# A two-block forward pass: the down products of the experts in four passes of 256 columns, with three quarters of the second block's projections under them

## The reference, cut to what matters

```python
hid = silu(einsum('becd,edf->becf', xs, w_gate)) * einsum('becd,edf->becf', xs, w_up)
eo  = einsum('becf,efd->becd', hid, w_down)          # w_down: 16 x 2048 x 1024
x   = x + zeros.at[bidx, idx].add(gates * eo)
x   = rms_norm(x, final_g)                           # end of the first block
h   = modulate(rmsnorm(x, g_pre_mix), shift, scale)  # start of the second
q, k, v, z, gl = split_proj(h @ w_in_2)              # 1024 x 7168
kv_c = hc @ w_in_2[:, 1024:3072]                     # keys and values of 256 context tokens
```

## Time and profile before

| | us |
|---|---|
| median of 2 timed runs (2216.74 to 2218.97) | 2217.85 |
| the profiled execution | 2217.74 |
| its span, first to last instruction | 2215.9 |
| PE busy | 1514.1 |
| DVE busy | 742.5 |
| ACT busy | 429.9 |
| mean transfer rate over the span, GB/s | 361 |

### The profile page before, as it was taken

The page is one execution under the profiler, slowest core; times in us unless marked ns, Lnnn a source line. Parts: engine busy times, 40 slices in busy tenths (PEclk is TensorE's granted clock), DMA queues, the critical chain, the costliest instruction groups (busy, mean ns, idle before and its releaser), DMA issues.

```text
span 2215.9 us, 24722 instructions
## 1 busy us (share of the span) xinstructions
PE 1514.1 (68%) x10356; PEld 613.8 (28%) x10356; DVE 742.5 (34%) x1862; ACT 429.9 (19%) x998; POOL 309.4 (14%) x290
## 2 busy tenths in 40 slices
PE   9998676776565655659855988897686854434445
PEld 7554133221111111113211334454333620100001
DVE  5831100000000000000000235445767686776774
ACT  1430100000000000000000106443414542221222
POOL 0110000000000000000000000001343445444351
PEclk9999888877777777889977999898686975565555
DMA  9699989999999999999455824357999999999997
GB/s 408 269 423 383 421 348 399 402 392 428 427 429 428 428 428 427 428 420 425 197 232 232 335 88 176 114 190 293 382 418 416 421 420 420 421 421 420 421 420 308
DMA packets 76750, 800.89 MB, mean 361 GB/s; under 512 B 9088, under 2 KB 9216, under 8 KB 10592
## 3 DMA queue, kind: packets, MB, share of 16 engines
q1 hardware_dynamic: 39008, 530.66, 57.4%
q0 software_dynamic: 37632, 268.65, 29.3%
HBM read 798.03 MB, written 1.05 MB: 361 GB/s over the span
## 4 chain that ended last, share of the span: by engine, by line
DMA 42%; PE 42%; DVE 9%; ACT 3%; issue 2%; POOL 0%; SPq 0%; DVEq 0%; another core or an unknown queue 0%; ACTq 0%; POOLq 0%
DMA AR<-in_peer_uv,AR 13%; DMA AR<-in_w_up 12%; DMA AR<-in_w_down 10%; PE PS L413 5%; DMA AR<-in_w_gate 5%; PE PS L699 5%; PE PS L860 5%; PE PS L772 5%; PE PS L424 4%; PE PS L738 4%; DVE AR L1638 3%; PE PS L996 3%; PE PS L953 2%; PE PS L535 1%; PE PS L781 1%
## 5 line engine op out<-in xcount | busy, mean ns | idle before, releaser
L699 PE MATMUL PS<-AR 128*32 128x512 f32 x2048 | 330.1, 782 | 202.9 <-DMA AR<-in_w_up 129.3
L2072 POOL DMA_INDIRECT AR<-in_peer_uv,AR x256 | 293.6, 1147 | 1071.8 <-DVE AR L1629 772.7
L996 PE MATMUL PS<-AR 32*32 32x512 f32 x4032 | 224.7, 907 | 288.5 <-ACT AR L2008 285.2
L1638 DVE CUSTOM_DVE_ANT_0 AR<-AR 128x1024 f32<-128x1024 f32 x256 | 309.2, 1222 | 158.8 <-DMA AR<-in_peer_uv,AR 158.2
L738 PE MATMUL PS<-AR 128*32 128x512 f32 x1024 | 177.9, 756 | 131.4 <-DMA AR<-in_w_down 130.8
L1292 DVE TENSOR_TENSOR AR<-AR,PS 128x512 f32<-128x512 f32 x16 | 11.0, 687 | 593.4 <-PE PS L699 593.4
L699 PEld LDWEIGHTS PS<-AR 128*32 128x32 f32 x2048 | 64.7, 127 | 447.0 <-DMA AR<-in_w_up 208.8
L996 PEld LDWEIGHTS PS<-AR 32*32 32x32 f32 x4032 | 39.1, 124 | 428.8 <-ACT AR L2008 415.2
L413 PE MATMUL PS<-AR 128*128 128x512 f32 x288 | 136.1, 629 | 7.3 <-ACT AR L1704 4.0
L1320 DVE COPY AR<-PS 128x512 f32<-128x512 f32 x8 | 5.5, 692 | 315.8 <-PE PS L738 315.8
L860 PE MATMUL PS<-AR 128*128 128x512 f32 x224 | 106.4, 630 | 0.1
(11 more groups left out here) (312 smaller groups left out, 1441.6 us busy)
## 6 DMA issues: line engine op xcount, KB each, us to landing
AR<-in_w_up SPq DMA_DIRECT2D x64, 2048.0 KB, 20.8
AR<-in_w_down SPq DMA_DIRECT2D x64, 2048.0 KB, 15.9
AR<-in_w_gate SPq DMA_DIRECT2D x63, 2048.0 KB, 21.1
AR<-in_w_in SPq DMA_DIRECT2D x15, 2048.0 KB, 10.4
AR<-in_w_ada SPq DMA_DIRECT2D x12, 2048.0 KB, 12.8
AR<-in_w_in SPq DMA_DIRECT2D x14, 1024.0 KB, 12.7
AR<-in_w_out SPq DMA_DIRECT2D x6, 2048.0 KB, 8.0
AR<-in_peer_w_query SPq DMA_DIRECT2D x5, 2048.0 KB, 7.6
```

The lines of the kernel that those rows point to most:

```text
L699: x = pe.matmul(PS[32 * q:32 * q + 32, bk, :], XS[e][:, j, :], src[:, q * 512:(q + 1) * 512], start=(j == 0), stop=(j == 7), skip_group_ch ...
L996: x = pe.matmul(PS[c:c + 32, ACC[a][g], :], DI[t, p, r, :], AR[t, off + 1024 + m * 512:off + 1536 + m * 512], start=(h == 0 and p == 0), s ...
L1638: v.tensor_tensor_reduce(rows, rows, HB[:, a, :], 1.0, 0.0, MULT, ADD, DOT[:, ix, k:k + 1]).then_inc(*w.hit("dot", ix, k))
L2072: pool.indirect_dma_start(out=AR[:, off:off + 2048], out_offset=None, in_=D["peer_uv_2"], in_offset=bass.IndirectOffsetOnAxis(ap=EI[:, ix, ...
```

## The change

Four passes over 256 output features instead of two over 512. A down block is still 2 MB: 16 products of 32x256, four blocks for a quad, 16 in a pass (64 in all, as before). After each of the first three passes a quarter of the features (two chunks of 128) is final and turned (`quarter_turn`).

The early projections are cut in three. `piece(m, n, q)` is 4 products of 128x512 (2 chunks, 2 token halves) over quarter q, for projection m and column half n; its weights for both n are one transfer of 1 MB (`pre`). Pass 1 runs the pieces of quarter 0 for k, q, v, z2, z0; pass 2 those of quarter 1; pass 3 those of quarter 2, and all three quarters of ga and gs: 10, 10 and 22 pieces. ACT copies the first quarter's part, DVE adds the later ones. The shift's sums use all four groups of 32 columns. `rest` has only the last quarter: 4 products instead of 8, from weights of 1 MB.

One table, `PHASE`, made by `expert_order`, gives the order for PE, DVE, ACT and SP. All pieces use the two half slots S50 and S51 in turn. The norms work on 256 features where they worked on 512, and the sum of the shift's shares is copied and paired behind the last piece.

The context products move too: each context weight has P6 for itself, loaded after the up weights of experts 4 to 7, and is used in four pieces, one behind each gate chunk of experts 5 to 8. P6 joins the ring at expert 9.

The core of the diff:

```diff
-        QUADS = [[0, 1, 2, 3], [2, 3, 0, 1]]
-        AHEAD = [(m, n) for m in ("k", "q", "v", "z2", "z0", "ga", "gs") for n in range(2)]
+        QUADS = [[0, 1, 2, 3]] * 3 + [[2, 3, 0, 1]]
+        AHEAD = [[]] + [[(m, q) for m in ("k", "q", "v", "z2", "z0")] for q in range(3)]
+        AHEAD[3] += [(m, q) for m in ("ga", "gs") for q in range(3)]
...
+                        upto = total * (b - 2) // 13 if b > 2 else 0
...
+                        upto = (10 * (b - 2) // 5 if b < 8 else 10 + 12 * (b - 7) // 8) if b > 2 else 0
...
-                        if (name, c) == ("gate", 1):
-                            if e in (4, 5):
-                                context_keys(e - 4, 2)
-                            elif e in (6, 7):
-                                context_values(e - 6, 1)
+                        if name == "gate" and 5 <= e < 9:
+                            context_piece(e - 5, c)
...
-                for s2 in range(2):
+                for sh in range(4):
                     for g in range(4):
-                        x = pe.matmul(PS[32 * g:32 * g + 32, b, :], HDT[4 * q + g][:, 2 * sh + s2, fq * 32:(fq + 1) * 32], IN[key][:, g, s2, :],
-                                      start=(blk == 0 and s2 == 0), stop=(blk == 7 and s2 == 1), skip_group_check=True)
+                        x = pe.matmul(PS[32 * g:32 * g + 32, b, 0:256], HDT[4 * q + g][:, sh, blk * 32:(blk + 1) * 32], IN[key][:, g, sh, :],
+                                      start=(blk == 0 and sh == 0), stop=(blk == 3 and sh == 3), skip_group_check=True)
...
+            def piece(m, n, q):
+                key = ("pre", m, q)
+                r = PAIRS.index(m)
+                for a in range(2):
+                    b, before = banks.use("part", m, n, q, a)
+                    w.wait_ge(*before)
+                    w.wait_ge("in", *key)
+                    w.wait_ge("half", q)
+                    for j in range(2):
+                        x = pe.matmul(PS[:, b, :], HT[:, 2 * q + j, a * 128:(a + 1) * 128], IN[key][:, n, j, :], start=(j == 0), stop=(j == 1))
...
-                    for j in range(4, 8):
-                        x = pe.matmul(PS[:, to[n][0], :], HT[:, j, a * 128:(a + 1) * 128], IN[key][:, n, j - 4, :], start=False, stop=(j == 7))
+                    for j in (6, 7):
+                        x = pe.matmul(PS[:, to[n][0], :], HT[:, j, a * 128:(a + 1) * 128], IN[key][:, n, j - 6, :], start=False, stop=(j == 7))
...
-                        if (e, key, c) == (4, "upw", 0):
-                            w.wait_ge("mm", "xsa", 7)
+                        if (e, key, c) == (9, "upw", 0):
                             turn[0], ids[0] = 4, [*ids[0][turn[0] % 4:], *ids[0][:turn[0] % 4], P6]
...
+                elif 4 <= e < 8:
+                    if e == 4:
+                        w.wait_ge("mm", "xsa", 7)
+                    load(P6, ("ctx_k", e - 4) if e < 6 else ("ctx_v", e - 6), weight("w_kv_2", e - 4), 8, 512)
...
+            def early(t, m, q):
+                load((S50, S51)[t % 2], ("pre", m, q), D["w_in_2"][PAIRS.index(m), q].rearrange("p (n j c) -> p n j c", n=2, j=2), 2, 2, 512)
```

More of the change, by code:

```diff
@@ new lines, in spread, with quarter_turn @@
+                x.then_inc(*w.hit("mm", "spread", dc, i, also=[("mm", "y", dc)] * (i == 3)))
+            def quarter_turn(dc):
+                b, before = banks.use("half", dc)
+                w.wait_ge(*before)
+                for a in range(2):
+                    w.wait_ge("xg", dc, a)
+                    for j in (2 * dc, 2 * dc + 1):
+                        x = pe.transpose(PS[:, b, (j % 2 * 2 + a) * 128:(j % 2 * 2 + a + 1) * 128], XG[:, a, j * 128:(j + 1) * 128], ident)
+                x.then_inc(*w.hit("mm", "half", dc))
@@ L1373, in vector @@
-            block_out(1, 0)
-            gained(1, 0)
-            block_out(1, 1)
+                v.tensor_scalar(XN[:, a, 768:1024], XG[:, a, 768:1024], s4, None, MULT).then_inc(*w.hit("xn4", a))
+            for stage, *x in PHASE:
+                if stage == "bias":
+                    bias_sum()
+                elif stage == "spread":
+                    dc, i = x
+                    gathered(dc, i)
+                    if i == 3 and dc < 3:
+                        for a in range(2):
+                            block_out(dc, a)
+                            gained(dc, a)
+                elif stage == "turn":
+                    quarter_turn(*x)
+                    if x == [2]:
+                        first_sums()
+                elif stage == "piece":
+                    piece(*x)
@@ L1883, in scalar @@
+            for stage, *x in PHASE:
+                if stage == "spread" and x[1] == 3 and x[0] < 3:
+                    for a in range(2):
+                        squares(x[0], a)
+                        gained_squares(x[0], a)
+                elif stage == "piece":
+                    piece(*x)
             act.activation(s8[:, 2:3], ident[:, 0:1], ACT.Sqrt)
             for a in range(2):
-                squares(1, a)
+                squares(3, a)
                 if a == 0:
-                    gained_squares(1, 0)
+                    gained_squares(3, 0)
@@ L2165, in down @@
             def down(dc, i, blk):
                 q = QUADS[dc][i]
[L2167 to L2171 removed]
+                ring(("down", dc, q, blk), D["w_down"][dc, q, blk].rearrange("p (g s n) -> p g s n", g=4, s=4), 4, 4, 256)
@@ L2186, in sync @@
-            ids[0], turn[0] = [2, 3, 4], 0
-            for i in range(4):
-                for blk in range(8):
-                    d = 8 * i + blk
-                    if d % 2 == 0 and d // 2 < len(AHEAD):
-                        early(d // 2, (SA0, SA1, S50, S51, SA0, SA1)[d // 2] if d < 12 else (S50, S51)[d // 2 % 2])
-                    down(1, i, blk)
-            user[5] = user[S51]
+                    elif x == [1, 0, 0]:
+                        user[S50] = user[S51] = user[5]
+                        ids[0], turn[0] = [2, 3, 4], 0
@@ L2194, in sync @@
+                    down(*x)
+            user[5] = user[S50]
             turn[0], ids[0] = 0, RING
```

347 lines of the change are left out of this document (176 added, 171 removed).

## The result

| | before | after |
|---|---|---|
| median of 2 timed runs, us | 2217.85 | 2123.34 (2119.81 to 2126.86) |
| the profiled execution | 2217.74 | 2126.86 |
| its span | 2215.9 | 2125.1 |

The ratio is 0.957, interval 0.950 to 0.965: 94.5 us less, where 96 were forecast (2122, range 2100 to 2166). A second and a third set of runs of the same kernel gave 2125.18 and 2123.94 (0.958 and 0.959 of before). So the sum holds to about 3 us. The rest of this part asks whether its terms do.

What follows compares the result with a forecast made beforehand. Bound by SP's blocked queue in experts and second down pass, where transfers and PE idle, then by PE in the remaining projections. Savings 17 + 39 + 0 + 40 = 96 take 2217.7 to 2122 us, range 2100 to 2166.

Steps and rivals of the forecast that it cites:

- Experts, 17: Expert stretch: moving the context products into pieces with their own weight slot saves 17 us, bounds 20 won to 5 lost.
- the 19.8 us of lost transfer time: Experts, 300 to 480 us: transfers busy only 0.89 of the time; 19.8 us the most that could be removed.
- Down passes, 39: Down products, first to last: 432.3 us become 392.6; 39 us saved, bounds 44 and 25.
- Block 51: First down block of the last pass with pieces: arrives at 1092.4; from there PE, not transfers, bounds, with 115.5 us of work.
- The unknown product: Down block of 32 output columns by 256, shown by no row: taken as 1.79 us, between 1.72 and 7.17.
- Rival D: Down passes: narrow 256-column products run one after another, 7.17 us a block, 247 us more, 2369; chance 0.03.
- Rival C: Last down pass: SP's held queue lives on, nine loads each baring 9.5 us, 86 us in all, 2208; chance 0.04.
- rival E: Passes 2 and 3: pieces not hidden because products run at 1.2 GHz, 120 us, 2240; chance 0.03, half as mild as 60.
- Seams, 0 within 2: After the last piece: later bias sum costs about 2 us, quarter-wide norms take about as much less; zero, within 2.
- The price of 0.13 us per change of shape: Down passes: each switch between product shapes costs 0.13 us; 28 more switches, 3.6 us if all on the path.
- Remaining projections, 40 = 27 + 4 + 9: Fourteen halved projections behind the down products: 27 us from eight, 4 from z0, ga, gs, 9 from three; bounds 49 and 20.
- A pair takes 26.0 us instead of 12.67: Second down pass from 1081 us: early loads hold SP's queue, baring 9.5 us of latency every second block.

Runs made afterwards that it cites:

- the last experiment: The changed kernel with one of the two chunks left out in the pieces of ga and gs, all transfers kept: 2110.37 us, ratio 0.9510.

## Why the prediction was right, and where it was not

The total was right (2122 for 2123.3), and that was in part luck: errors of opposite sign in its terms met. Against the profiled execution, 90.8 us, the terms are 5.2 too large in all: 3.6 too small for the experts, and 4.3, 2.6 and 2.5 too large for the down passes, the seams and the remaining products, with 0.6 won behind them.

*Experts, 17.* Measured 20.6, 19.3 at the end when done alone. Four slots did under the pieces, and the transfers never stood still: share 1.01 from 240 to 480 us. So the 19.8 us of lost transfer time were the better value, and the 2.8 taken off them stood on no row. The end of this stretch differs by 3.6 us between profiles of one kernel (795.6, 792.0 and 792.5), so it is 20.6 to 24.2 in the three.

*Down passes, 39.* Measured 34.7. Block 51, forecast at 276.2 us behind the first product, starts at 278.4 (1074.0 - 795.6). The sum by bytes is 2.2 us short. From there PE took 119.2 us instead of 116.4, and what is over lies at the beginning. The timeline of the changed kernel there:

```profile
1074.01 2.68 PE L782 MATMUL PS<-AR 128*32 128x256 f32 x32 [2.49 <-DMA AR<-in_w_down]
1077.86 9.10 PE L817 MATMUL PS<-AR 128*128 128x512 f32 x16 [1.17 <-issue]
```

After a wait of 2.49 us the block takes 2.68 instead of 1.91, the pieces come 1.17 later and take 9.10 instead of 7.13. From the block's start to the bias sum behind the pieces it is 12.9 us (1074.0 to 1086.9), two steps later 8.9 (1098.4 to 1107.3): 4.0 us over. The regular steps behind it are shorter than the terms made them, 9.79 against 1.79 + 2 x 3.63 + 0.86 = 9.91, though the bias sum is 1.00 instead of 0.86; eleven of them give 1.3 us back. That the transfers bound passes 2 and 3, that the work turns over at this block, and that no down block is waited for behind it, all came as forecast. The last pass begins at 1063.4 instead of near 1060 and ends at 1193.2 instead of near 1191, with a clock of 0.97 from this block on where 1.00 was forecast.

*The unknown product.* 32 columns by 256 took 1.73 per block in the chain, inside the 1.72 to 7.17 that stood as bounds, and at the end that was chosen. Rival D is gone: such products do run side by side. Rival C is gone as well, though its nine waits are there, and rival E too: the clock was 0.96 and 0.97 in the passes with pieces. The drain at a change of tiling mode, which the Trainium skill's "TensorEngine Tiling (Array Packing)", Key Properties, speaks of, adds nothing to what was priced: the whole step is shorter than its terms. The price of 0.13 us per change of shape was a misreading of the chain. By the starts in the timeline of the changed kernel a block between two pieces takes 1.86 us (1057.05 to 1058.91), one behind a bias sum 1.83 (1051.58 to 1053.41); most of the 0.13 lies in where the chain ends a group.

*Seams, 0 within 2.* Measured +2.6. Of the two waits in the rows below, the first, for VectorE's add and copy behind the last piece, is the one that was named. The second is for VectorE's line 1402, the sum of the bias block, and was not named. Line 470 behind it are filler products (`keep_busy`, nobody reads their result). Before, PE had made them by 1254.6, 0.8 us after VectorE had the norm ready (1253.8); now they begin later and hold the turns of the norm back from 1199.6 to 1202.1, 2.5 us. So 1.7 of the 2.6 us stand behind these fillers; leaving some of them out was not tried. These two rows are the timeline of the changed kernel's seam:

```profile
1194.67 1.10 PE L838 MATMUL PS<-AR,PK 128*128 128x512 f32 x2 [1.46 <-DVE AR L1382]
...
1198.53 3.72 PE L470 MATMUL PS<-PK 128*128 128x256 f32 x16 [1.91 <-DVE AR L1402]
```

*Remaining projections, 40 = 27 + 4 + 9.* Measured 28.0, then 1.5, with 1.1 given back behind it, then 9.1. The first and last group came to within 1 us. The mistake is in the middle: of the 10.6 us taken from three products there 0.4 is left instead of 4. The prediction had named both waits that would grow, for the layer norm of z2 and for ScalarE, and then took a share of 40 per cent on no row. Its own rows would have given less. From the scores product that begins this stretch to the end of the norm it is 19.3 us before (1345.4 to 1364.7) and 18.7 after (1264.8 to 1283.5). From `zmix` to the first product of bs, which waits for ScalarE, it is 17.6 before and 18.3 after. Neither got shorter for PE's doing less, so all that could be won was the time between them, the 1.9 us of room that the prediction had read: 0.1 is left of it. What PE did sooner fell into the waits and the slower work right behind them: 4.09 for the norm, `zmix` at 3.48 instead of 2.05, and 6.45 instead of 3.96 for ScalarE.

*To what the gain was credited.* No step of the sum failed so that the total shows it, but the credit was wrong. "A pair takes 26.0 us instead of 12.67" was read rightly as a fault of SP's order, and the gain was then booked under "down passes" of the change. The runs show that moving one issue behind two others wins 74.7 us with the passes as they were, and that with the context part it reaches the changed kernel's time. What the title of the change speaks of, four passes with pieces under three of them, adds nothing that these runs can tell: 1.4 and 0.6 us for it by the medians of two sets, 0 and 3 against it by the ratios. The prediction could have seen it: a pair of blocks took 12.67 us before the loads were held and 26.0 behind them, six times over the earlier trace rows. Six times the difference is 80 us, for the order of SP's queue alone; the one-line edit showed 75.

That both designs take the same time fits what PE does in them. Both run the same projection products. In four passes the first pass has 16 blocks with nothing beside them and the middle ones have transfers at 1.00, so PE idles 57.4 us in all before down products (the page's row of line 782), and then has 119 us of its own in the last. In two passes with the order mended, the first has 32 blocks with nothing beside them, but the second fills PE for 186.5 of 187 us and the transfers for 0.95. The balance of the two was computed for neither before it was measured, so it is no rule.

## What to carry to other kernels

Before a change to the structure is credited with removing a wait, take the wait away by the smallest edit that does it and time that; here one issue moved behind two others in a queue that goes in order won 75 of the 95 us. In such a queue, put a load whose slot is not free yet behind those whose slots are. Work moved under another stage pays only where the engine idles there, and where the profile already shows the engine waiting for another at the end of a stretch, look for the room before that wait: work taken from the engine there wins about that and no more (1.5 of 10.6 us here, of which 1.1 were given back behind it).

## What the runs showed of the hardware that was not expected

- A wait of 2.49 us cost more than itself again: the block behind it took 2.68 us instead of 1.91 and the next sixteen rows 9.10 instead of 7.13, 2.7 us together, with a gap of 1.17 between them. The granted clock goes with it, as three short stretches of the changed kernel show (columns of the earlier trace rows): 0.68, then 0.76, then 1.00.

```profile
1074.00:1077.00 3.00, 2.68 (x32) 1.11 (x32) 0.00 (x0) 0.00 (x0) 0.00 (x0) 0.68 1.01 426
1077.00:1087.00 10.00, 9.14 (x20) 3.86 (x24) 2.06 (x3) 0.00 (x0) 0.00 (x0) 0.76 1.00 428
1087.00:1097.00 10.00, 10.00 (x59) 4.80 (x58) 3.09 (x5) 0.00 (x0) 0.00 (x0) 1.00 0.86 334
```

  In the last experiment a wait of 2.69 was followed by a block of 3.62, 1.7 more; behind 0.39 and 0.48 the next took 1.93 and, for eight rows, 3.67, no more than without a wait. Behind a wait of 6.45 in the mixer sixteen rows took 9.71 instead of 7.13, 2.6 more. The prediction priced a small gap at its length.
- Narrow products of 256 columns have no price of their own: 32 rows of them take 1.73 us in the chain, as 16 rows of 512 columns do (1.72 and 1.85), though there are twice as many instructions and weight loads.
- The gathers take 685 us in every kernel here, from 684.7 to 686.5, wherever they begin (1425.7 to 1530.1). All that moves the first gather moves the end by as much.
